# Input tile as the outer loop in the first output blocks behind five norms of a decoder step

## The chip, the cores and the metric

The kernel runs on one core of a Trainium2 chip. The metric is the device time of one execution in microseconds (us), lower is better; of several executions the median counts. All times "at" a point are us from the span's start in one profiled execution.

## The reference, cut to what matters

One inference step of a two-layer decoder for 512 prompt tokens and 64 sample tokens (8 sequences of 8), in float32, width 1024. The parts that the change touches are these matrix products, each behind a norm or a gate that makes its input:

```python
def rms_norm(x, g):
    xf = x.astype(jnp.float32)
    y = xf * lax.rsqrt(jnp.mean(xf * xf, axis=-1, keepdims=True) + EPS)
    return (y * g.astype(jnp.float32)).astype(x.dtype)
...
        x = x + rms_norm(sq_relu_mlp(h, W['w_up'][i], W['w_down'][i]), W['norm_ff_post'][i])
        x = x + jax.nn.sigmoid(x @ W['ple_gate'][i]) * (ple[i] @ W['ple_proj'][i])
...
    h = rms_norm(x, kv_in_g)
    ckr = h @ w_dkv
...
    cq = rms_norm(h @ w_dq, q_norm_g)
    q = (cq @ w_uq).reshape(B, T, N_HEADS, QK_NOPE + QK_ROPE)
```

The second layer's MLP is `square(relu(h @ w_up)) @ w_down` with 4096 hidden columns.

## The kernel before, in words

Activations lie with the feature on the partitions and the 576 tokens in the free dimension, as 8 tiles of 128 features, and the tokens are worked in two halves, h = 0 and 1, of 288. A **unit** is one output block: 128 output features of one half. Its product runs over the input tiles k (8, or 6 behind the query norm, where the rank is 768), and to keep float32 precision each k takes three matmuls (`three`, L2285 to L2290): weight high part by input high part, high by low, low by high. So a unit has 24 matmuls (18 behind the query norm, 12 in the MLP's down products).

TensorE works through all units in an order written out by hand. Before the change, most products run the units one after another, with k inside (`product`, L2318, and `up`, L2549). For the first unit that reads a new input, TensorE waits at each k for that tile's low part (`a_lo`); the later units find all tiles there. Two earlier places already have k as the outer loop over three units (`product_by_rows`, L2348, and `ff_up_by_rows`, L2468).

A unit starts when two more things are there:

- **Its bank.** Four PSUM banks serve the units in turn, so unit n waits until unit n - 4 has been read out by VectorE (`bank_free`). VectorE runs its own fixed order: for the gate units it is `gate` (L1954: sigmoid from ScalarE times an embedding, L1957, which frees the bank, then the addition to X, L1960), and in the MLP's up units the square of the relu (`u_square`, L1881, L1884). In that order stand also the updates of X (L1622) and the low parts of the next input (L1590, L1594).
- **Its weights.** A part of 128 weight columns (in the down products 256 columns of a shorter k) is split by ScalarE into its high part WH (L651) and by GpSimd into its low part WL (L1302). Four parts fit in the ring. The part for a later unit can be split only when the last unit that reads the old part in that slot has ended, and stands in the fixed order of ScalarE and GpSimd, among squares, sums and scalings of the norms.

Where weights serve both halves, the units come as groups: in the gate product units 0 to 3 are h 0 and 4 to 7 are h 1 of the same four parts, in dkv likewise, in dq units 0, 1 and 2, 3, in uq 0 to 3 and 4 to 7; in the MLP's up product 0 to 3 and 4 to 7. The `total` of a norm (L2309, L2315) is one matmul with a matrix of ones that sums the squares over the partitions. After it comes a root on ScalarE (L687), a reciprocal on VectorE (L1615 or L1610), scaling on GpSimd (L1338), the update of X (L1622) or nothing, the high part on ScalarE (L701, L703) and the low part on VectorE (L1590, L1594).

In the MLP, the chain of one up unit is: relu (ScalarE, L972), square (VectorE, L1884, frees the bank), high part (ScalarE, L976), low part (GpSimd, L1489). The buffer of the squares holds two, so the square of unit n waits for the low part of unit n - 2. For units 4 to 7 GpSimd does one weight part (L1302) and one low part (L1489) in turn.

Of the kernel before, what the change touches and what calls it, by code (L numbers as in the profile page):

```python
# [35 lines left out]
KT = D // P  # L36
TP, TS = 512, 64
T = TP + TS
H = T // 2
# [37 lines left out]
RAW0, DENSE0, UNIT0, UNITS = {}, {}, {}, {}  # L77
# [46 lines left out]
def slab_tiles(phase, j):  # L124

    return 8 if phase[:3] == "ple" else 1 if (phase, j) == ("dkv", 2) else 2


TILES = {p: [(h, j, t) for g in groups for h in range(2) for j in g for t in range(slab_tiles(p, j))]
         for p, groups in GROUPS.items()}  # L130
# [69 lines left out]
A = Order([(v, h, m) for v, h, n in SPLITS for m in range(n)])  # L200
# [19 lines left out]
BANKS = 4  # L220
# [21 lines left out]
def decoder_step(nc, io):  # L242
    with ExitStack() as ctx:
# [3 lines left out]
        def sem(name):  # L247
            return ctx.enter_context(nc.semaphore(name))

        bank = [ctx.enter_context(nc.psum_tensor(f"bank{i}", [P, 512], F32)) for i in range(8)]  # L250
# [57 lines left out]
        unit_done, bank_free = sem("unit_done"), sem("bank_free")  # L308
# [5 lines left out]
        a_hi, a_lo, x_done, sc_done = sem("a_hi"), sem("a_lo"), sem("x_done"), sem("sc_done")  # L314
# [5 lines left out]
        def half(t, m, h):  # L320
            return t[:, m, h * H:(h + 1) * H]
# [285 lines left out]
        def part_width(d):  # L607

            kt, n = slab_shape(*DENSE[d][1:])
            return kt, n // (PART0[d + 1] - PART0[d])  # L610
# [1673 lines left out]
        def _(pe):  # L2284
            def three(out, wsl, hl, first, last):  # L2285

                (wh, wl), (xh, xl) = wsl, hl
                nc.tensor.matmul(out, wh, xh, start=first, stop=False)  # L2288
                nc.tensor.matmul(out, wh, xl, start=False, stop=False)  # L2289
                return nc.tensor.matmul(out, wl, xh, start=False, stop=last)  # L2290

            def wpart(d, k, t):

                w = part_width(d)[1]
                q, c = divmod(t * P, w)
                r, a = (PART0[d] + q) % WRING, k * w + c
                return WH[:, r, a:a + P], WL[:, r, a:a + P]

            def rows(src, k, h):

                return half(src[0], k, h), half(src[1], k, h)

            def ready(d, t, i=None):
                w = PART0[d] + t * P // part_width(d)[1] + 1
                pe.wait_ge(lo_done, w if i is None else w + 2 * RING * i)

            Asrc, Bsrc = (AH, AL), (BH, BL)
# [10 lines left out]
            def product(phase, v, first=0, last=None, src=None):  # L2318

                kt = part_width(DENSE0[phase])[0]  # L2320
                for n, (h, j, t) in list(enumerate(TILES[phase]))[first:last]:
                    u, d = UNIT0[phase] + n, DENSE0[phase] + j
                    b = bank[u % BANKS][:, 0:H]
                    ready(d, t)
                    pe.wait_ge(bank_free, u + 1)
                    for k in range(kt):
                        if v and n == [x[0] for x in TILES[phase]].index(h):
                            pe.wait_ge(a_lo, A(v, h, k))
                        ins = three(b, wpart(d, k, t), rows(Asrc, k, h) if src is None else src(k, h), k == 0,
                                    k == kt - 1)  # L2330
                    ins.then_inc(unit_done, 1)
# [13 lines left out]
                        pe.wait_ge(lv_sq, m + 1)  # L2345
                        nc.tensor.matmul(dst, ones[:, :], LVS[:, m, :], start=first, stop=last).then_inc(lv_sum, 1)

            def product_by_rows(phase, v, units):  # L2348

                h = TILES[phase][0][0]  # L2350
                for k in range(KT):
                    pe.wait_ge(a_lo, A(v, h, k))
                    for n in range(units):
                        _, j, t = TILES[phase][n]
                        u, d = UNIT0[phase] + n, DENSE0[phase] + j
                        if k == 0:
                            ready(d, t)
                            pe.wait_ge(bank_free, u + 1)
                        ins = three(bank[u % BANKS][:, 0:H], wpart(d, k, t), rows(Asrc, k, h), k == 0, k == KT - 1)
                        if k == KT - 1:  # L2360
                            ins.then_inc(unit_done, 1)

            def turn_input(e):
# [181 lines left out]
            def mlp(layer):  # L2545
                phase, sty, stx, st = f"mlp{layer}", f"y{layer}", f"x{2 * layer + 1}", f"m{layer}"
                d0, u0, b0 = DENSE0[phase], UNIT0[phase], UP * NCH * layer

                def up(i, first, last):  # L2549
                    for n in range(first, last):  # L2550
                        h, j, t = n // 4, n % 4 // 2, n % 2
                        ready(d0 + j, t, i)
                        pe.wait_ge(bank_free, u0 + n + 1 + CHUNK * i)
                        for k in range(KT):
                            if type(i) is int and i == 0 and n % 4 == 0:
                                pe.wait_ge(a_lo, A(f"ff{layer}", h, k))
                            ins = three(bank[(u0 + n) % BANKS][:, 0:H], wpart(d0 + j, k, t), rows(Asrc, k, h), k == 0,
                                        k == KT - 1)
                        ins.then_inc(unit_done, 1)

                def down(i, first, last):
                    for n in range(first, last):
                        h, j, t = n // 8, 2 + n % 8 // 4, n % 4
                        ready(d0 + j, t, i)
                        pe.wait_ge(bank_free, u0 + UP + n + 1 + CHUNK * i)
                        for k in range(FC):
                            if n % 8 == 0:
                                pe.wait_ge(u_lo, b0 + up_n(h, k) + 3 + UP * i)
                            ins = three(bank[(u0 + n) % BANKS][:, 0:H], wpart(d0 + j, k, t), rows(Bsrc, k, h), k == 0,
                                        k == FC - 1)  # L2570
                        ins.then_inc(unit_done, 1)

                def turn_p(kt):
                    if kt == 0:
                        pe.wait_ge(p_in, 80 * (layer + 1))
                    else:
                        pe.wait_ge(p_lo, 6 * layer + 3)
                    for b in range(4):
                        nc.tensor.transpose(bank[6][:, b * P:(b + 1) * P], p_stage[:, b, kt * P:(kt + 1) * P],
                                            ident[:, :])  # L2580
                    nc.tensor.transpose(bank[7][:, 0:TS], p_stage[0:TS, 4, kt * P:(kt + 1) * P], ident[0:TS, 0:TS])\
                        .then_inc(p_turned, 1)

                up(0, 0, 2)
                total(sty, 1)
                up(0, 2, 8)
                down(0, 0, 16)
                with pe.Fori(1, NCH - 1) as i:
                    up(i, 0, 8)
                    down(i, 0, 16)  # L2590
                up(NCH - 1, 0, 8)
                down(NCH - 1, 0, 3)
                for h in range(2):
                    total(stx, h)
                down(NCH - 1, 3, 10)
                total(st, 0)
                turn_p(0)
                down(NCH - 1, 10, 13)
                turn_p(1)
                down(NCH - 1, 13, 16)  # L2600
                pe.wait_ge(p_lo, 6 * layer + 6)
                product(f"ple{layer}", None, src=lambda k, h: (BH[:, 2 * k + h, 0:H], BL[:, 2 * k + h, 0:H]))
                total(st, 1)

            product("gate0", "g0", 0, 1)
            total("m0", 1)
            product("gate0", "g0", 1)
            product("dkv", "kv", 0, 5)
            total("x2", 0)
            product("dkv", "kv", 5, 7)  # L2610
            total("x2", 1)
            product("dkv", "kv", 7)
            product("dq", "mx", 0, 1)
            for h in range(2):
                total("ck", h)
            product("dq", "mx", 1, 9)
            total("cq", 0)
            product("dq", "mx", 9)

# [14 lines left out]
                nc.tensor.transpose(bank[5][0:n, 0:DR], KR[0:DR, t0:t0 + n], ident[0:DR, 0:DR])\  # L2634
                    .then_inc(kv_turned, 1)

            product("uq", "cq", 0, 2)
            total("cq", 1)
            product("uq", "cq", 2, 4)
            pe.wait_ge(rope_in, 16)  # L2640
            pe.wait_ge(dve_step, KR_STEP)
            rot(0, KR)
            product("uq", "cq", 4, 8)
            for j in range(5):
                turn_kv(j)
                product("uq", "cq", 8 + 3 * j, 11 + 3 * j)
# [99 lines left out]
            for h in range(NH):  # L2746
                e = h % 2
                ins = nc.tensor.matmul(bank[5][:, h * TS:(h + 1) * TS], DUP[:, e, :],
                                       QR[:, h // 2, TP:T], start=True, stop=True)
# [32 lines left out]
            g0 = RAW0["cache"]  # L2782
# [122 lines left out]
            for hd in range(NH):  # L2905
# [5 lines left out]
                for k in range(4):  # L2911
                    a = k * 512 + (hd % 4) * P
                    ins = nc.tensor.matmul(bank[hd % 4][:, 0:TS], RAW[:, g % RING, a:a + P],
                                           LATS[:, k, hd].rearrange("p s t -> p (s t)"), start=k == 0, stop=k == 3)
# [74 lines left out]
```

## Time and profile before

| | |
|---|---|
| runs | 1956.98, 1959.21, 1967.64 us; median 1959.21 us |
| profiled execution | 1963.1 us, span 1960.8 us |
| TensorE (PE) busy | 91% of the span |
| GpSimd (POOL) busy | 52% |
| VectorE (DVE) busy | 47% |
| ScalarE (ACT) busy | 38% |
| mean granted TensorE clock | 0.952 of full |

A row of the timeline has the start, the duration, the engine, the line of the kernel, the operation, output and input tiles, how many instructions were merged, and in brackets the idle time of that engine just before with what ended it. PE rows of matmuls start 0.13 us apart when the engine runs without a pause at full clock; their durations overlap.

### The profile page before, as it was taken

How to read it: one execution, taken by the hardware profiler on the slowest of the kernel's cores; microseconds unless marked ns; L12 is line 12 of the kernel's file. 1: busy time of each engine (PE TensorE's matmuls, PEld its weight loads, DVE VectorE, ACT ScalarE, POOL GpSimd, SP SyncE). 2: the span in 40 equal slices, each digit the busy share in tenths (PEclk: the TensorE clock that was granted, in tenths of full speed). 3: DMA queues.
4: the chain of work that ended last, by engine and by line, in shares of the span. 5: the costliest groups of instructions: out<-in, count | busy, mean ns of one | idle time of the engine just before them, and what ended most of it. 6: DMA issues, size and time to landing. Idle time of an engine off the chain costs nothing.

```text
span 1960.8 us, 33358 instructions
## 1 busy us (share of the span) xinstructions
PE 1792.0 (91%) x12372; PEld 1609.7 (82%) x12372; DVE 923.3 (47%) x2170; ACT 739.9 (38%) x1454; POOL 1019.3 (52%) x739
## 2 busy tenths in 40 slices
PE   5994699999999799889999899999979999999978
PEld 4992699998899798888866566565969999999978
DVE  4687789943423325673344444444162222222283
ACT  4445444445444343632132333333232232322332
POOL 3784689986799784754210000000465555555662
PEclk9996899999999899998998899999889999999989
DMA  4521245544355341312102145555412222222201
GB/s 117 154 82 46 86 130 172 169 166 130 108 172 158 123 151 33 111 49 78 54 1 65 33 124 166 151 155 166 141 44 87 86 80 73 82 85 74 78 22 49
DMA packets 183288, 198.54 MB, mean 101 GB/s; under 512 B 32985, under 2 KB 138035, under 8 KB 183170
## 3 DMA queue, kind: packets, MB, share of 16 engines
q1 hardware_dynamic: 178144, 190.94, 31.5%
q10 hardware_dynamic: 5026, 6.02, 1.0%
q8 instruction: 75, 1.23, 0.3%
q14 instruction: 43, 0.35, 0.1%
HBM read 192.14 MB, written 4.79 MB: 100 GB/s over the span
## 4 chain that ended last, share of the span: by engine, by line
PE 66%; POOL 14%; DVE 11%; ACT 4%; issue 4%; DMA 1%; ACTq 0%; SPq 0%; POOLq 0%; DVEq 0%
PE bank L2288 16%; PE bank L2289 16%; PE bank L2290 16%; POOL WL L1302 7%; PE bank L2831 4%; PE bank L2865 3%; PE bank L2789 3%; DVE X L1622 2%; POOL acc L1328 2%; DVE AL L1590 2%; ACT WH L651 1%; PE bank L2730 1%; DVE AL L1594 1%; POOL R L1380 1%; PE bank L2711 1%
## 5 line engine op out<-in xcount | busy, mean ns | idle before, releaser
L1302 POOL TENSOR_TENSOR WL<-RAW,WH 128x1024 fp32r<-128x1024 f32 (+1 forms) x283 | 670.7, 2380 | 738.2 <-ACT WH L651 736.5
L2288 PE MATMUL bank<-AH,WH 128*128 128x288 f32 x2112 | 646.1, 306 | 65.4 <-DVE AL L1590 40.9
L2289 PE MATMUL bank<-AL,WH 128*128 128x288 f32 x2112 | 633.4, 300 | 0.0
L2290 PE MATMUL bank<-AH,WL 128*128 128x288 f32 x2112 | 632.6, 300 | 0.0
L2288 PEld LDWEIGHTS bank<-AH,WH 128*128 128x128 f32 x2112 | 406.9, 193 | 81.5 <-DVE AL L1590 36.5
L2289 PEld LDWEIGHTS bank<-AL,WH 128*128 128x128 f32 x2112 | 407.8, 193 | 0.9
L2290 PEld LDWEIGHTS bank<-AH,WL 128*128 128x128 f32 x2112 | 407.2, 193 | 0.0
L651 ACT ACTIVATE WH<-RAW 128x1024 fp32r<-128x1024 f32 (+1 forms) x283 | 293.5, 1045 | 301.3 <-PE bank L2290 283.9
L2288 PE MATMUL bank<-BH,WH 128*128 128x288 f32 (+1 forms) x1120 | 339.8, 303 | 25.6 <-DVE Y L1772 14.4
L2289 PE MATMUL bank<-BL,WH 128*128 128x288 f32 (+1 forms) x1120 | 336.1, 300 | 0.0
L2290 PE MATMUL bank<-BH,WL 128*128 128x288 f32 (+1 forms) x1120 | 336.0, 300 | 0.0
L2288 PEld LDWEIGHTS bank<-BH,WH 128*128 128x128 f32 x1120 | 213.2, 190 | 31.1 <-issue 27.7
L2289 PEld LDWEIGHTS bank<-BL,WH 128*128 128x128 f32 x1120 | 213.4, 191 | 1.4
L2290 PEld LDWEIGHTS bank<-BH,WL 128*128 128x128 f32 x1120 | 213.0, 190 | 1.5
L1699 DVE SCALAR_TENSOR_TENSOR bank<-S,taps,bank 128x224 f32<-128x224 f32 x464 | 134.8, 364 | 0.0
L1884 DVE TENSOR_TENSOR prod<-R,bank 128x288 f32<-128x288 f32 x64 | 29.1, 454 | 182.8 <-ACT R L972 111.2
L1893 DVE TENSOR_TENSOR Y<-Y,bank 128x288 f32<-128x288 f32 x112 | 50.7, 452 | 112.5 <-PE bank L2290 112.4
L1328 POOL TENSOR_TENSOR acc<-acc,sq 128x288 f32<-128x288 f32 x100 | 82.0, 823 | 32.5 <-ACT sq L669 26.7
L1338 POOL TENSOR_TENSOR scaled<-Y,R 128x288 f32<-128x288 f32 x76 | 69.2, 921 | 38.6 <-DVE X L1622 15.0
L1489 POOL TENSOR_TENSOR BL<-prod,BH 128x288 fp32r<-128x288 f32 x64 | 51.6, 811 | 61.0 <-ACT BH L976 61.0
L1772 DVE TENSOR_TENSOR Y<-Y,bank 128x288 f32<-128x288 f32 x112 | 49.5, 448 | 60.8 <-PE bank L2290 60.6
L2831 PE MATMUL bank<-Y,prod 128*64 128x256 f32 x640 | 76.1, 384 | 0.4 <-ACT Y L1212 0.4
(258 smaller groups left out, 2106.8 us busy)
## 6 DMA issues: line engine op xcount, KB each, us to landing
RAW<-in_w_up SPq DMA_DIRECT2D x48, 1024.0 KB, 5.5
RAW<-in_w_down SPq DMA_DIRECT2D x48, 1024.0 KB, 5.0
RAW<-in_cache_kv_latent SPq DMA_DIRECT2D x128, 256.0 KB, 2.8
RAW<-in_conv_pw SPq DMA_DIRECT2D x16, 512.0 KB, 7.5
RAW<-in_conv_pw SPq DMA_DIRECT2D x8, 1024.0 KB, 4.9
RAW<-in_ple_gate SPq DMA_DIRECT2D x8, 1024.0 KB, 5.0
RAW<-in_cache_k_rope SPq DMA_DIRECT2D x128, 32.0 KB, 2.8
RAW<-in_w_o SPq DMA_DIRECT2D x4, 1024.0 KB, 4.8
```

The lines of the kernel that those rows point to most:

```text
L651: nc.scalar.activation(split_part(WH, d, q), raw_part(d, q), ACT.Copy).then_inc(hi_done, 1)
L1302: nc.gpsimd.tensor_tensor(split_part(WL, d, q), raw_part(d, q), split_part(WH, d, q).bitcast(F32), ALU.subtract).then_inc(lo_done, 1)
L1328: nc.gpsimd.tensor_tensor(dst, dst, src, ALU.add).then_inc(acc_done, 1)
L1338: nc.gpsimd.tensor_tensor(scaled[:, SC(st, h, m) % 2, :], src, R2[:, h, :], ALU.mult).then_inc(sc_done, 1)
L1489: nc.gpsimd.tensor_tensor(half(BL, m, h), prod[:, n % 2, :], half(BH, m, h).bitcast(F32), ALU.subtract).then_inc(u_lo, 1)
L1699: nc.vector.scalar_tensor_tensor(out=run if c < CW - 1 else out, in0=src, scalar=w, in1=run, op0=ALU.mult, op1=ALU.add).then_inc(conv_late, 1)
L2288: nc.tensor.matmul(out, wh, xh, start=first, stop=False)
L2289: nc.tensor.matmul(out, wh, xl, start=False, stop=False)
L2290: return nc.tensor.matmul(out, wl, xh, start=False, stop=last)
L2789: ins = nc.tensor.transpose(bank[4 + c][:, q * P:(q + 1) * P], src[:, q * CL + c * P:q * CL + (c + 1) * P], ident[:, :])
L2831: ins = nc.tensor.matmul(bank[0][64 * g:64 * g + 64, 0:256], q, k, start=c == 0, stop=c == 4)
L2865: ins = nc.tensor.matmul(dst[g], SPT[:, k, 64 * g:64 * g + 64], src[:, b * CL:(b + 1) * CL], start=k == 0 and (j > 0 or g == 1), stop=k == 1)
```

## The change

`product_by_rows` gets a first unit and the right number of input tiles, and is used at five more call sites; the MLP of layer 1 gets a function of the same form, used twice. Around them the rest of each product is cut to fit. Two `total`s move: those of "ck" from behind dq unit 0 to behind dq unit 1, and that of "y1" half 1 from behind up unit 1 to behind up unit 2. Nothing changes on the other engines, and no instruction is added or taken away on TensorE.

```diff
-            def product_by_rows(phase, v, units):
-
-                h = TILES[phase][0][0]
-                for k in range(KT):
+            def product_by_rows(phase, v, units, first=0):
+
+                h, kt = TILES[phase][first][0], part_width(DENSE0[phase])[0]
+                for k in range(kt):
                     pe.wait_ge(a_lo, A(v, h, k))
-                    for n in range(units):
+                    for n in range(first, first + units):
                         _, j, t = TILES[phase][n]
                         u, d = UNIT0[phase] + n, DENSE0[phase] + j
                         if k == 0:
                             ready(d, t)
                             pe.wait_ge(bank_free, u + 1)
-                        ins = three(bank[u % BANKS][:, 0:H], wpart(d, k, t), rows(Asrc, k, h), k == 0, k == KT - 1)
-                        if k == KT - 1:
+                        ins = three(bank[u % BANKS][:, 0:H], wpart(d, k, t), rows(Asrc, k, h), k == 0, k == kt - 1)
+                        if k == kt - 1:
                             ins.then_inc(unit_done, 1)
...
+                def up_by_rows(first, units):
+                    h = first // 4
+                    for k in range(KT):
+                        pe.wait_ge(a_lo, A(f"ff{layer}", h, k))
+                        for n in range(first, first + units):
+                            j, t = n % 4 // 2, n % 2
+                            if k == 0:
+                                ready(d0 + j, t, 0)
+                                pe.wait_ge(bank_free, u0 + n + 1)
+                            ins = three(bank[(u0 + n) % BANKS][:, 0:H], wpart(d0 + j, k, t), rows(Asrc, k, h), k == 0,
+                                        k == KT - 1)
+                            if k == KT - 1:
+                                ins.then_inc(unit_done, 1)
...
-                up(0, 0, 2)
+                up_by_rows(0, 3)
                 total(sty, 1)
-                up(0, 2, 8)
+                up(0, 3, 4)
+                up_by_rows(4, 4)
                 down(0, 0, 16)
...
-            product("gate0", "g0", 1)
-            product("dkv", "kv", 0, 5)
+            product("gate0", "g0", 1, 4)
+            product_by_rows("gate0", "g0", 4, 4)
+            product("gate0", "g0", 8)
+            product_by_rows("dkv", "kv", 4)
+            product("dkv", "kv", 4, 5)
...
-            product("dq", "mx", 0, 1)
+            product_by_rows("dq", "mx", 2)
             for h in range(2):
                 total("ck", h)
-            product("dq", "mx", 1, 9)
+            product("dq", "mx", 2, 9)
...
-            product("uq", "cq", 0, 2)
+            product_by_rows("uq", "cq", 2)
             total("cq", 1)
...
-            product("uq", "cq", 4, 8)
+            product_by_rows("uq", "cq", 4, 4)
```

## Rows read from the trace of the kernel before

**Rows 1.** The page, busy time of each engine.
```profile
PE 1792.0 (91%) x12372; PEld 1609.7 (82%) x12372; DVE 923.3 (47%) x2170; ACT 739.9 (38%) x1454; POOL 1019.3 (52%) x739
```

**Rows 2.** Waits of PE: line, what it waited for, us in total, times, longest us.
```profile
PE bank L2288 <- DVE AL L1590: 40.9, 28, 8.2
...
PE bank L2288 <- DVE AL L1594: 13.0, 12, 5.5
```

**Rows 3.** Timeline of gate0: VectorE frees banks (L1957), PE, one GpSimd weight part.
```profile
747.67 0.53 DVE L1957 TENSOR_TENSOR R<-prod,S 128x288 f32<-128x288 f32 x1 [0.44 <-ACT prod L1046]
...
753.49 0.45 DVE L1957 TENSOR_TENSOR R<-prod,S 128x288 f32<-128x288 f32 x1
...
754.35 0.45 DVE L1957 TENSOR_TENSOR R<-prod,S 128x288 f32<-128x288 f32 x1
...
757.90 0.29 PE L2288 MATMUL bank<-AH,WH 128*128 128x288 f32 x1
...
759.54 2.39 POOL L1302 TENSOR_TENSOR WL<-RAW,WH 128x1024 fp32r<-128x1024 f32 x1 [0.83 <-ACT WH L651]
...
764.30 0.30 PE L2288 MATMUL bank<-AH,WH 128*128 128x288 f32 x1
```

**Rows 4.** Windows: us; busy PE, PEld, DVE, ACT, POOL; granted clock; DMA.
```profile
748.10:755.00 6.90, 4.95 (x18) 4.20 (x19) 6.66 (x15) 2.50 (x7) 1.89 (x2) 0.52 0.00 0
795.90:799.30 3.40, 3.25 (x14) 3.25 (x15) 3.40 (x6) 1.97 (x6) 2.34 (x4) 0.52 0.76 228
831.00:834.40 3.40, 3.40 (x24) 3.40 (x25) 3.30 (x9) 3.40 (x9) 0.00 (x0) 1.00 0.00 0
1441.00:1451.30 10.30, 6.17 (x25) 5.82 (x26) 5.73 (x7) 2.76 (x5) 6.76 (x5) 0.51 0.33 103
```

**Rows 5.** Timeline of dkv: last gate unit's bank freed, PE's longest wait, unit 4 starts.
```profile
794.33 0.40 PE L2288 MATMUL bank<-AH,WH 128*128 128x288 f32 x1 [2.72 <-DVE AL L1590]
...
794.63 0.44 DVE L1957 TENSOR_TENSOR R<-prod,S 128x288 f32<-128x288 f32 x1
...
807.82 0.29 PE L2288 MATMUL bank<-AH,WH 128*128 128x288 f32 x1
```

**Rows 6.** Timeline of dq: PE's first matmul.
```profile
831.00 0.37 PE L2288 MATMUL bank<-AH,WH 128*128 128x288 f32 x1 [2.91 <-DVE AL L1590]
```

**Rows 7.** Timeline of uq: PE's last wait, GpSimd, total, first wait of half 1, weight part, unit 8.
```profile
885.82 0.61 PE L2288 MATMUL bank<-AH,WH 128*128 128x288 f32 x1 [1.04 <-DVE AL L1590]
...
887.43 1.82 POOL L1302 TENSOR_TENSOR WL<-RAW,WH 128x768 fp32r<-128x768 f32 x1
...
891.02 0.56 PE L2315 MATMUL bank<-acc,ones 128*128 128x288 f32 x1
...
898.00 0.37 PE L2288 MATMUL bank<-AH,WH 128*128 128x288 f32 x1 [0.42 <-DVE AL L1590]
...
905.60 1.84 POOL L1302 TENSOR_TENSOR WL<-RAW,WH 128x768 fp32r<-128x768 f32 x1 [2.72 <-ACT WH L651]
...
912.57 0.40 PE L2288 MATMUL bank<-AH,WH 128*128 128x288 f32 x1
```

**Rows 8.** Timeline of the MLP's first chunk: GpSimd's weight parts and low parts, PE, a square.
```profile
1442.08 2.56 POOL L1302 TENSOR_TENSOR WL<-RAW,WH 128x1024 fp32r<-128x1024 f32 x1
...
1448.42 2.37 POOL L1302 TENSOR_TENSOR WL<-RAW,WH 128x1024 fp32r<-128x1024 f32 x1
...
1452.48 0.40 PE L2315 MATMUL bank<-acc,ones 128*128 128x288 f32 x1
...
1456.69 0.40 PE L2288 MATMUL bank<-AH,WH 128*128 128x288 f32 x1 [0.40 <-POOL WL L1302]
...
1464.47 0.45 DVE L1884 TENSOR_TENSOR prod<-R,bank 128x288 f32<-128x288 f32 x1 [0.47 <-ACT R L972]
...
1475.65 0.81 POOL L1489 TENSOR_TENSOR BL<-prod,BH 128x288 fp32r<-128x288 f32 x1
...
1482.74 0.29 PE L2288 MATMUL bank<-BH,WH 128*128 128x288 f32 x1
```

## The prediction

> **What bounds the kernel now.** I read the page first: TensorE is busy 91% of the span and no other engine over 52% [rows 1]. So the change can only give or take where TensorE stands still. The waits of TensorE say where that is: for low parts of inputs behind a norm or a gate it stood 40.9 + 13.0 us in 40 waits, the longest 8.2 us [rows 2]. The seven new calls stand at some of these waits. The idea of the change is plain in them: the first unit has 0.4 us of work per input tile (three matmuls, 0.13 us apart), and a group of four has 1.6 us.
>
> That is one half of the question. The other is what the later units of a group need at k = 0: a free bank and a weight part. Units one after another ask for these 3.2 us apart (24 matmuls), a group asks for all at once, before its second k. TensorE is in order, so one missing bank stops the whole group. So I read each site in the timeline of VectorE and GpSimd, and looked up when the bank and the part come. I call three matmuls a triple, 0.40 us.
>
> A third reading is the clock. After waits it stood at 0.51 to 0.52, that is 1.2 GHz: for 6.9 us in gate0, for 3.4 us in dkv after a wait of 2.72 us, for 10.3 us in the MLP. But in dq, after a wait of 2.91 us, it stayed at 1.00, or 2.4 GHz [rows 4 to 6]. A stretch of 3.4 us at 1.2 GHz loses about 1.5 us of work.
>
> **Gate0, units 4 to 7: +6.6 us.** Unit 5 needs unit 1's bank, unit 6 that of unit 2, unit 7 that of unit 3. VectorE frees them at 748.20, 753.94 and 754.80, because gate(1) stands behind four of the eight updates of X, and gate(2) and gate(3) behind all of them [rows 3]. So TensorE does three triples up to 754.4, and reaches the second k only after 754.9. From there it has 29 triples: 11.6 us, to 766.5. The long idle stretch before it puts some 3.4 us of that at 1.2 GHz: +1.5, to 768.0. Before, unit 8 started at 764.30 [rows 3]: +3.7. Then the weights: the four parts that this group reads are all in the ring, and are now freed within its last round. A unit's end to the new part in its place takes ScalarE and GpSimd 4.1 us (unit 5 ended at 757.90, its successor's part at 761.93 [rows 3]). Unit 4 ends 1.2 us before the group, so unit 8 waits 2.9 us. Before, this part came 5 us too early and cost nothing: the cover was units 5 to 7, which now end with unit 4. The later parts come every 2.4 us, faster than the 3.2 us of a unit.
>
> **Dkv, units 0 to 3: +0.4 us.** Unit 3 needs the bank of gate unit 15, free at 795.07 [rows 5]. 29 triples and the same slow stretch of 3.4 us give 808.2; before, unit 4 started at 807.82. The weights serve half 1 as well, so there is no refill.
>
> **Dq, units 0 and 1: 0.** The low parts come faster than TensorE uses them once the first is there at 831.00 [rows 6]: 0.3 us at most, and the waits that follow are for GpSimd's weight parts behind the "ck" norm. The two "ck" totals come 3 us later, but VectorE is still at its low parts then. With that cover gone it would cost up to 3 us.
>
> **Uq, units 0, 1 and 4 to 7: -5.6 us.** Here the banks come from plain copies and are free. In the first pair TensorE follows the low parts to 885.8 and needs two more triples: 886.6. Total "cq" 1 waits for GpSimd's last sum, 887.43 [rows 7], and runs at 887.6 instead of 891.02. Of these 3.4 us, units 2 and 3 lose 1.2: their parts are the two that GpSimd does from 887.43, ready at 889.3 and 891.1, so unit 3 ends at 894.2. VectorE copies it and comes to the first low part of half 1 at 895.4; before TensorE had it at 898.00 [rows 7]. Then 24 triples, 9.6 us, each k of 1.6 us above the 1.2 us between low parts: 905.0. The refill lag is about 3.1 us with these shorter parts (1.84 instead of 2.39 us), so unit 8 starts at 907.0, against 912.57 [rows 7]. GpSimd's and VectorE's work overlap more here; I take nothing for it, up to 2 us.
>
> **MLP, units 0 to 2 and 4 to 7: +8.1 us.** Unit 1 needs a weight part that GpSimd ends at 1444.64, unit 2 one that it ends at 1450.79 [rows 8], both behind the scalings of the norm in its order and independent of TensorE. So the second k starts after 1451; 22 triples from 1450.9 are 8.8 us, and the slow stretch 1.7 more (none, if the clock were up; 3, if it took the 6 us seen before 1451.3 [rows 4]): 1461.4. Total "y1" 1 ran at 1452.48: it is 8.9 us late. So is GpSimd's low part of unit 0 (it waits until ScalarE has had unit 1's end), and behind it the weight part of unit 3, which TensorE got at 1456.69. The norm's half 1 chain hangs on both, and moves by 8.4. Unit 7 needs unit 3's bank, whose square stands behind four updates of X: 1464.47 + 0.45 [rows 8], now 1473.3. From there 29 triples: 1484.9, against 1482.74: +2.2. The group takes back most of the delay. Then 2.9 for the refill as above. And a pile: for units 4 to 7 GpSimd does a weight part and a low part in turn, 2.37 + 0.81 us, and the square of unit 6 waits for the low part of unit 4, that of unit 7 for unit 5's. Counted from the group's end, weights are there at 2.9, low parts 3, 4, 5 at 3.7, 6.9, 10.1, so the banks of 6 and 7 are free at 7.4 and 10.6. The down units (1.6 us each) want them at 6.1 and, after that wait, 9.1: 1.4 + 1.6 = 3.0. Before, the squares ran 3.2 us apart and hid this.
>
> **Sum.** 6.6 + 0.4 + 0 - 5.6 + 8.1 = 9.5. The two refill waits of 2.9 us can bring a slow stretch: 0 by dq's wait, 1.5 to 1.7 by dkv's [rows 4 to 6]; I take 0.8 for each, since they are alike in length: 11.1 us. The profiled execution's 1963.1 becomes 1974.2; it is 3.9 above the median of 1959.2, so the forecast is 1970.3. A measurement here can tell some 0.5%, 9.8 us, from no change.
>
> **Rivals.** First, faster: banks and parts come in time, and each group runs without a stop. Gate0: 744.7 + 12.8 + 2.9 = 760.4, -3.9. Dkv: 789.8 + 12.8 = 802.6, -5.2. Uq -5.6. MLP: a total 3.5 earlier and a group like gate0's, -7.4. Together -22, 1937. It decides where the bank of unit n - 4 is free when the group starts. For it speak the 53.9 us of rows 2; against it the stamps 754.80, 795.07 and 1450.79. The Trainium skill, Perfetto Trace Analysis, Matmul Optimizations, wants matmuls back-to-back in batches; by that rule this rival comes true. The trace agrees in uq alone.
>
> Second, small: the order is as I say, but the clock stays up and the squares keep pace. Without the slow stretches (1.5, 1.5, 1.7, 1.6) and the pile (3.0) it is +1.8; with half of them, +6: 1961 to 1965. For it speaks dq's clock of 1.00 after 2.91 us.
>
> Third, uq gives nothing: its earlier totals meet GpSimd's work, or a later wait takes them back. Then the losses stand alone, +16.7, 1976. The Trainium skill, TensorE: Matmul & The Clock Gate, Loop structure matters more than you think, puts k inside and the outputs outside to keep matmuls dense; by that rule no group should gain. Against it: in uq, 24 triples took 13.1 us from 898.00 to the transposes before 912.57, 3.5 more than their work.
>
> **How the numbers follow.** Forecast 0.38, at 1970.3 (its own range 1966 to 1975); uq nothing 0.12; small 0.37; faster 0.13, which holds also gains smaller than -22. Slower is 0.50, same 0.37, faster 0.13. The range leaves out the faster rival and a little above: 1958 to 1978.
>
> **What would show it.** In gate0: a wait of the second and third triple for VectorE's L1957, and one of about 2.9 us for POOL WL L1302 at unit 8. In dkv one wait for L1957 of 3 to 4 us. In uq the total at about 3 us less behind unit 0's first k, and unit 8 some 5 us earlier in relation to it. In the MLP two waits for POOL WL in the first round, 9 and 6 us, the total some 9 us later, then waits for the squares, L1884, in the down units. I am wrong if TensorE's waits at L2288 for VectorE's low parts vanish with nothing in their place, or if the clock stays at 1.00 through the MLP's first rounds.

## The result and the profile after

The changed kernel took 1984.19 us (median of 4 runs, 1980.6 to 1986.34) beside 1961.72 us of the kernel before (4 runs): a ratio of 1.0116, with a 95% interval of 1.0086 to 1.0145. The forecast was 1970.3, with a range up to 1978. So the direction was right, and the loss was 22 us instead of 11. The two profiled executions lie closer together: 1980.6 against 1963.1, +17.5. In a later comparison with more runs (below, the changed kernel once more) the ratio was 1.0062, 1.0037 to 1.0086. These two intervals only touch, at 1.0086, and that is part of what had to be explained.

The page of the changed kernel, busy time and the granted clock over the span. TensorE is as busy as before [rows 1], within 3 us:

```profile
span 1978.3 us, 33358 instructions
PE 1794.8 (91%) x12372; PEld 1613.6 (82%) x12372; DVE 933.5 (47%) x2170; ACT 739.4 (37%) x1454; POOL 1018.5 (51%) x739
```

The waits of PE at the line of the products (what it waited for, us in total, times, longest):

```profile
PE bank L2288 <- POOL WL L1302: 32.8, 11, 9.5
PE bank L2288 <- DVE AL L1590: 21.0, 9, 8.4
...
PE bank L2288 <- DVE R L1957: 11.6, 4, 4.7
PE bank L2288 <- DVE AL L1594: 9.5, 7, 5.5
...
PE bank L2288 <- DVE prod L1884: 4.0, 3, 1.7
```

The change did what it says. The waits for low parts went from 53.9 us in 40 waits [rows 2] to 30.5 us in 16. In their place came 22.8 us more for weight parts (they were 10.0), 11.6 us for banks behind the gates' last step (L1957) and 4.0 us for banks behind the squares (L1884): 38.4 us for 23.4.

The sites, in PE's timeline: gate0 (three stops), dkv (two), dq:

```profile
747.23 0.58 PE L2288 MATMUL bank<-AH,WH 128*128 128x288 f32 x1 [3.08 <-DVE R L1957]
...
752.95 0.58 PE L2288 MATMUL bank<-AH,WH 128*128 128x288 f32 x1 [4.66 <-DVE R L1957]
...
769.84 0.41 PE L2288 MATMUL bank<-AH,WH 128*128 128x288 f32 x1 [2.68 <-POOL WL L1302]
...
798.60 0.37 PE L2288 MATMUL bank<-AH,WH 128*128 128x288 f32 x1 [0.70 <-DVE R L1957]
...
802.42 0.58 PE L2288 MATMUL bank<-AH,WH 128*128 128x288 f32 x1 [3.19 <-DVE R L1957]
...
839.74 0.61 PE L2288 MATMUL bank<-AH,WH 128*128 128x288 f32 x1 [2.81 <-DVE AL L1590]
```

Then uq (its total and its two stops for weight parts), and in the MLP's first chunk the stops of units 1, 2, 3 and 7 and of the first down unit:

```profile
896.89 0.75 PE L2315 MATMUL bank<-acc,ones 128*128 128x288 f32 x2 [0.66 <-POOL acc L1328]
...
898.65 0.40 PE L2288 MATMUL bank<-AH,WH 128*128 128x288 f32 x1 [1.01 <-POOL WL L1302]
...
916.20 0.40 PE L2288 MATMUL bank<-AH,WH 128*128 128x288 f32 x1 [1.06 <-POOL WL L1302]
...
1454.94 0.61 PE L2288 MATMUL bank<-AH,WH 128*128 128x288 f32 x1 [9.50 <-POOL WL L1302]
...
1461.06 0.61 PE L2288 MATMUL bank<-AH,WH 128*128 128x288 f32 x1 [5.03 <-POOL WL L1302]
...
1476.62 0.40 PE L2288 MATMUL bank<-AH,WH 128*128 128x288 f32 x1 [3.37 <-POOL WL L1302]
...
1484.45 0.37 PE L2288 MATMUL bank<-AH,WH 128*128 128x288 f32 x1 [1.66 <-DVE prod L1884]
...
1498.96 0.40 PE L2288 MATMUL bank<-BH,WH 128*128 128x288 f32 x1 [2.68 <-POOL WL L1302]
```

And the clock (window; busy time of the engines; granted clock; DMA), in gate units 8 and 9, behind dkv's waits and behind dq's:

```profile
771.30:774.30 3.00, 3.00 (x15) 3.00 (x14) 3.00 (x2) 0.25 (x1) 3.00 (x2) 0.51 0.18 41
798.60:807.00 8.40, 5.21 (x22) 5.01 (x23) 8.37 (x12) 6.26 (x15) 5.39 (x5) 0.68 0.37 118
839.70:846.00 6.30, 6.26 (x26) 6.27 (x27) 6.16 (x14) 3.77 (x9) 0.00 (x0) 0.51 0.00 0
```

Now the time between like points of the two timelines. Each shift is taken against the point before it:

| stretch, up to | before | after | shift in it | forecast |
|---|---|---|---|---|
| total "m0" | 734.16 | 733.07 | -1.1 | 0 |
| gate unit 8 | 764.30 | 769.84 | +6.6 | +6.6 |
| gate units 8 to 15 (clock) | | | +1.65 | +0.8 |
| dkv's group | | | +1.6 | +0.4 |
| dq, to total "cq" 0 | 867.78 | 878.52 | +1.9 | 0 |
| uq unit 8 | 912.57 | 916.20 | -7.1 | -5.6 |
| first page transposition, behind the attention heads | 1121.11 | 1131.49 | +6.8 | 0 |
| MLP, first unit | 1434.60 | 1444.88 | -0.1 | 0 |
| MLP, ninth down unit | 1495.39 | 1514.58 | +8.9 | +8.1 and +0.8 (clock) |
| end | | | -1.7 | 0 |

Eight of the ten lines are within 1.7 us of the forecast, and dq is 1.9 off. The one that stands out, +6.8 us, is in the attention heads, between two stages that the change touches: not one instruction is changed there.

### The profile page after: what moved, and what is told of

Same layout as the page of the kernel before. It is cut to its first block, busy times and chain, and to the rows that moved or that the text cites. A ratio compares the mean times of both kernels' runs of the same rounds, so it can differ in the third digit from the quotient of the medians.

```text
span 1978.3 us, 33358 instructions
## 1 busy us (share of the span) xinstructions
PE 1794.8 (91%) x12372; PEld 1613.6 (82%) x12372; DVE 933.5 (47%) x2170; ACT 739.4 (37%) x1454; POOL 1018.5 (51%) x739
## 4 chain that ended last, share of the span: by engine, by line
PE 66%; POOL 14%; DVE 10%; issue 4%; ACT 4%; DMA 1%; ACTq 0%; SPq 0%; POOLq 0%; DVEq 0%
PE bank L2288 16%; PE bank L2290 16%; PE bank L2289 16%; POOL WL L1302 8%; PE bank L2849 4%; PE bank L2883 3%; PE bank L2807 3%; POOL acc L1328 2%; DVE X L1622 2%; ACT WH L651 1%; PE bank L2748 1%; PE bank L2729 1%; POOL R L1380 1%; DVE AL L1590 1%; DMA RAW<-in_conv_pw 1%
## 5 line engine op out<-in xcount | busy, mean ns | idle before, releaser
L651 ACT ACTIVATE WH<-RAW 128x1024 fp32r<-128x1024 f32 (+1 forms) x283 | 293.2, 1044 | 296.3 <-PE bank L2290 277.8
L1884 DVE TENSOR_TENSOR prod<-R,bank 128x288 f32<-128x288 f32 x64 | 29.0, 453 | 193.5 <-ACT R L972 119.4
L972 ACT ACTIVATE R<-bank 128x288 f32<-128x288 f32 x64 | 26.3, 411 | 135.9 <-PE bank L2290 135.9
```

The source lines that it names most:

```text
L651: nc.scalar.activation(split_part(WH, d, q), raw_part(d, q), ACT.Copy).then_inc(hi_done, 1)
```

## First look: each part of the change alone

Four kernels, each with some of the new calls and the others as before. Uq alone:

```diff
-            product("uq", "cq", 0, 2)
+            product_by_rows("uq", "cq", 2)
...
-            product("uq", "cq", 4, 8)
+            product_by_rows("uq", "cq", 4, 4)
```

> Only the two groups of uq (units 0 and 1, units 4 to 7) are kept; the other five calls are undone. Theory A (the sites add up, and the 6.6 us lost between the first rope rotation and the cache pages came from where the clock and GpSimd's parts happened to fall): unit 8 of uq starts 5.6 to 7 us earlier behind total cq 0 than before, the attention heads take what they took before (954.90 to 1121.11, 166.2 us) or up to 7 us more by chance, time -7 to 0 us. Theory B (earlier totals of uq disturb the heads): the heads take 173 us, time about 0. Theory C (a group costs by itself, by switching bank at every triple): triples in the groups are longer than 0.40 us, time above before.

Measured: 1963.61 us, ratio 0.9999 (0.998 to 1.0018). In its trace, unit 8 comes 5.7 us earlier behind total "m0" than before (172.7 us against 178.4), as forecast. The heads take as much back: 172.5 us from the last projection of uq to the first page transposition, where the kernel before takes 1121.11 - 954.90 = 166.2. By itself this is theory B's picture; the kernels below decide against it.

What uq gains is less TensorE's idle time than its clock. Windows from total "cq" 0 to unit 8, the kernel before and this one:

```profile
867.78:912.57 44.79, 39.28 (x229) 35.94 (x229) 22.74 (x35) 13.96 (x25) 26.59 (x24) 0.85 0.21 44
```
```profile
867.98:907.06 39.08, 34.55 (x230) 32.01 (x230) 23.27 (x35) 13.78 (x25) 23.22 (x23) 0.96 0.21 41
```

Idle time (window less PE busy) went from 5.5 to 4.5 us, the busy time for the same matmuls from 39.3 to 34.6, at a mean clock of 0.85 and 0.96. So 1.0 of the 5.7 us are stops, and 4.7 are matmuls that run faster.

Gate0 alone:

```diff
-            product("gate0", "g0", 1)
+            product("gate0", "g0", 1, 4)
+            product_by_rows("gate0", "g0", 4, 4)
+            product("gate0", "g0", 8)
```

> Only the group of gate0 units 4 to 7 is kept. Theory A: three stops in it, of 3 and 4.7 us for L1957 and of 2.7 us for GpSimd's part at unit 8, a slow stretch after the first two and perhaps one after the third: +6.6 to +8.3 us at dkv, and that to the end: ratio 1.0034 to 1.0042. Theory C: more than that, in every triple. If a later stage takes the delay back: 0.

Measured: 1968.99 us, ratio 1.0036 (1.0017 to 1.0055), heads 166.2 us. Its three stops are those of the full change: 3.08, 4.67 and 2.68 us.

The MLP alone:

```diff
-                up(0, 0, 2)
+                up_by_rows(0, 3)
                 total(sty, 1)
-                up(0, 2, 8)
+                up(0, 3, 4)
+                up_by_rows(4, 4)
```

> Only the two groups of the MLP are kept. Theory A: stops of 9.5, 5.0, 3.4, 1.7, 2.7, 1.1 and 1.3 us as in the changed kernel, down unit 8 starts 8.9 us later behind the end of w_o than before, ratio 1.0045, heads unchanged. If the loss in the heads belongs to none of the sites, 0 to 7 us more by chance.

Measured: 1969.75 us, ratio 1.0039 (1.0018 to 1.0061), heads 170.8 us, and in the MLP the same stops within 0.03 us (9.50, 5.03, 3.37, 1.63, 2.67). Its heads are long as well, though nothing ahead of them differs from the kernel before.

Dkv and dq alone:

```diff
-            product("dkv", "kv", 0, 5)
+            product_by_rows("dkv", "kv", 4)
+            product("dkv", "kv", 4, 5)
...
-            product("dq", "mx", 0, 1)
+            product_by_rows("dq", "mx", 2)
             for h in range(2):
                 total("ck", h)
-            product("dq", "mx", 1, 9)
+            product("dq", "mx", 2, 9)
```

> Only the groups of dkv (units 0 to 3) and dq (units 0 and 1) are kept. Theory A: dkv 0.4 to 1.6 us, dq 0 to 2 us by how the clock falls, since a stop of 3 us for L1957 and one of 2.8 us for the low part each may or may not bring a slow stretch: +1 to +4 us, ratio 1.0005 to 1.002. With the clock at full the ck totals come 3 us late without a price; at half clock they come 6 us late and delay the norm by 2.

Measured: 1966.75 us, ratio 1.0015 (0.9997 to 1.0033), heads 171.8 us.

The four ratios add up to +0.89% (-0.01 + 0.36 + 0.39 + 0.15). So there is no cost that only the whole change has, beyond what the intervals allow, and the groups do not cost by themselves: a triple takes 0.40 us in them as elsewhere at full clock. The question was left with the heads. They took 166.2 us in two of the six traces and 171 to 173 in four, two with uq's calls and two without. So uq's earlier totals (theory B) are not what makes them long.

## What decides the heads: a near tie on a shared port

In heads 2 and 4 (counted from 0, so the third and the fifth) GpSimd makes two late weight parts back to back. In the middle of that, VectorE scales the softmax rows (L2112), on which TensorE waits. Both engines, kernel before, third head (start, duration, engine, line, operation; an entry of x2 holds two instructions):

```profile
1022.47 4.96 POOL L1302 TENSOR_TENSOR WL<-RAW,WH 128x1024 fp32r<-128x1024 f32 x2 [64.50 <-ACT WH L651]
1024.73 0.49 DVE L2112 TENSOR_SCALAR scaled<-scaled,tiny 128x512 f32<-128x512 f32 x1
...
1025.27 0.66 PE L2720 MATMUL bank<-ident,scaled 128*128 128x128 f32 x4 [0.49 <-DVE scaled L2112]
```

The same place in the changed kernel:

```profile
1026.52 2.00 ACT L651 ACTIVATE WH<-RAW 128x1024 fp32r<-128x1024 f32 x2
...
1027.65 4.65 POOL L1302 TENSOR_TENSOR WL<-RAW,WH 128x1024 fp32r<-128x1024 f32 x2 [66.09 <-ACT WH L651]
...
1028.89 0.70 ACT L1165 ACTIVATE scaled<-bank,tiny 128x512 f32<-128x512 f32 x1
...
1029.91 2.68 DVE L2112 TENSOR_SCALAR scaled<-scaled,tiny 128x512 f32<-128x512 f32 x1
...
1032.64 1.12 PE L2738 MATMUL bank<-ident,scaled 128*128 128x128 f32 x4 [2.68 <-DVE scaled L2112]
```

In both, VectorE's row starts 2.26 us behind the start of GpSimd's pair, 0.06 us before the row of the second part. Before, it got in between (0.49 us, and the pair took 4.96 us, 0.31 more than 4.65). After, it came in behind the second: 1029.91 + 2.68 = 1032.59, and the pair ended at 1032.30. The Trainium skill, SBUF — State Buffer, SBUF: two separate sides, says that the port pair these two engines share is an exclusive lock and the loser fully blocks. The rows agree with blocking; that a waiting instruction may or may not get in between two of the other engine's is not in it. I call it a tie, won if VectorE gets in between and lost if it waits for the second part.

The meeting itself is no accident. Both engines are released by ScalarE, in its fixed order: GpSimd by the end of the first WH part (L651), VectorE by the exponentials two instructions behind the second (L1165). In all ten traces that have the pairs, 20 meetings, the distance is 2.25 or 2.26 us; 7 were won and 13 lost. What decides one is below what the rows resolve.

The lost tie costs 2.2 us at once. Here it cost more behind, where TensorE's clock was slow. Windows of 11 us behind the tie, the kernel before and the changed kernel:

```profile
1025.00:1036.00 11.00, 10.73 (x53) 7.56 (x54) 5.25 (x19) 3.34 (x10) 2.43 (x1) 1.00 0.01 1
```
```profile
1032.00:1043.00 11.00, 10.36 (x28) 6.72 (x29) 3.43 (x13) 2.21 (x6) 0.30 (x1) 0.61 0.01 1
```

Over the whole of the heads, TensorE's idle time is 2.2 us longer in the changed kernel (15.0 and 12.8) and the busy time for the same 608 matmuls 4.6 us (140.8 and 136.2): together the 6.8.

The test takes the pair apart. The same four parts, one in each of heads 1 to 4:

```diff
-                if hd in (2, 4):
-                    hi_next(2)
+                if hd in (1, 2, 3, 4):
+                    hi_next(1)
```

First in the kernel before:

> The kernel before, but the four late weight parts that ScalarE and GpSimd make in heads 2 and 4 (two back to back) are made one in each of heads 1 to 4. The arithmetic is the same. Theory P (a near tie on the port that VectorE and GpSimd share decides the heads' length: in a head with two GpSimd parts back to back, VectorE's sum scaling either gets in between them, 0.49 us, or waits for the second, 2.68 us, and a wait of TensorE is followed by slower clock): VectorE's scaling waits no longer behind a second part, none of the heads' scalings is above about 1.5 us; the heads' part from the last projection of uq to the first page is 164 to 167 us (166.2 before), and the time is within 0.3% of before (1956 to 1966 us). Theory Q (the heads' length varies by itself, with the clock, whatever GpSimd does): this kernel's heads lie anywhere from 166 to 173 us, no shorter than those of other kernels.

Measured: 1960.14 us (12 runs, 1958.35 to 1963.45), ratio 0.9995 (0.9985 to 1.0004), heads 164.7 us. Its third head:

```profile
1024.77 2.35 POOL L1302 TENSOR_TENSOR WL<-RAW,WH 128x1024 fp32r<-128x1024 f32 x1 [16.80 <-ACT WH L651]
1026.88 0.52 DVE L2112 TENSOR_SCALAR scaled<-scaled,tiny 128x512 f32<-128x512 f32 x1
...
1027.45 0.66 PE L2720 MATMUL bank<-ident,scaled 128*128 128x128 f32 x4 [1.08 <-DVE scaled L2112]
```

No scaling in the heads took over 0.52 us. The spread of its 12 runs is as telling as the median: 5.1 us, where 20 runs of the kernel before on the same chip went from 1955.40 to 1968.38.

Then uq's two calls with the pair taken apart:

> The two uq groups of the change alone, with the late weight parts made one a head as in the kernel beside it. Theory P: the uq gain of 5.6 us is now kept: heads 164 to 167 us as there, and the time is 5 to 6 us under the kernel beside it (ratio to before 0.996 to 0.998). Theory Q: nothing is kept, heads 170 us and more, ratio to before 1.000, and the same time as the kernel beside it or more.

Measured: 1954.36 us, ratio 0.9967 (0.9951 to 0.9983), 5.8 us under the kernel beside it, as theory P said. The heads were 162.7 us, a little under the range that it gave. So uq's gain is real, and it reaches the time when the heads do not take it back.

The changed kernel, once as it is and once with the pair taken apart. (These texts count the heads from the first matmul on the norm's roots, 17.2 us further on: the 166.2 us of before are 149.0 so.)

> The changed kernel once more, for its time beside the others of this chip: 1980 to 1987 us. Theory P (the near tie on the shared port is lost once more in head 2 than before): its third head's scaling takes 2.68 us again, heads (last projection of uq to first page) 155 to 156 us against 149. Theory Q: the heads may be short this time, with the same kernel.

> The changed kernel with the late weight parts made one in each of heads 1 to 4 instead of two in heads 2 and 4. Theory P: no scaling of 2.68 us, heads 146 to 148 us, and 6 to 9 us under the changed kernel beside it (it gets rid of both lost ties): about 1976 us, ratio to before 1.006 to 1.009, which is near what was forecast for the change as a whole (9.5 + 1.6 us). Theory Q: as the changed kernel beside it, within 2 us.

Measured: as it is 1976.36 us (11 runs, 1973.94 to 1986.29), ratio 1.0062 (1.0037 to 1.0086), under the 1980 to 1987 that I had written; in its trace both ties are lost again (2.68 and 2.67 us), the heads 155.7 us. Taken apart: 1972.08 us (12 runs, 1969.78 to 1976.44), ratio 1.0036 (1.0014 to 1.0057), no scaling over 0.52 us, heads 147.6 us. The spans are 1980.6 and 1972.8, 7.8 us apart, within the 6 to 9 expected. The medians are 4.3 us apart and the ratio of 1.0036 lies under the 1.006 to 1.009 expected, so the forecast by medians was a miss. The 11 runs of the kernel as it is fall in two groups, four from 1982.9 to 1986.3 (the profiled one is among them) and seven from 1973.9 to 1979.6. That would fit runs that lose their ties and runs that win one or both; it is not shown, as only the profiled executions show a tie.

The 14 traces side by side; heads counted in this second way, the two scalings at GpSimd's pairs in order:

| kernel | scaling, head 2 | head 4 | heads |
|---|---|---|---|
| before; gate0 alone | 0.49 | 2.68 | 149.0; 149.1 |
| dkv and dq alone | 0.49 | 2.68 | 154.6 |
| MLP alone; its half 1 alone | 2.68; 2.69 | 2.68; 2.69 | 153.7; 153.7 |
| uq alone; changed, twice | 2.68 | 2.68 | 155.3; 155.8, 155.7 |
| dq alone; three groups (below) | 0.49 | 0.49 | 146.4; 146.5 |
| pair taken apart, four kernels | | | 145.5 to 147.6 |

All traces without a lost tie lie at 145.5 to 147.6 us, all with one or two at 149.0 to 155.8. Kernels with the very same program up to the heads (before, MLP alone, its half 1 alone) stand on both sides in head 2. So the tie is decided by something other than the calls of the change. Theory Q has its part too: with the ties the same, the heads took 149.0 and 154.6 us. In dkv and dq's trace the clock was 0.69 from 1022 to 1033 us, right behind a tie that it had won, where the kernel before has 1.00; what brought it down there stays open.

## Which calls gain, and how large a group may be

The change's own losses stand where a group asks for a bank or a part that is not there. If so, the same change with smaller groups, at the sites where TensorE waits for low parts alone, must gain:

```diff
-            product("dkv", "kv", 0, 5)
+            product_by_rows("dkv", "kv", 3)
+            product("dkv", "kv", 3, 5)
...
-            product("uq", "cq", 0, 2)
+            product_by_rows("uq", "cq", 2)
...
-            product("uq", "cq", 4, 8)
+            product_by_rows("uq", "cq", 4, 4)
...
                 up(0, 0, 2)
                 total(sty, 1)
-                up(0, 2, 8)
+                up(0, 2, 4)
+                up_by_rows(4, 3)
+                up(0, 7, 8)
```

> Only groups whose stages the traces show waiting for the norm's tiles rather than for weight parts: both uq groups as in the change, dkv with three units in the group instead of four (units 0 to 2), and in the MLP the group of four on the second half of the chunk alone (first three units of it), its first two units one by one as before; gate0 and dq as before. Theory A (each site's time is the wait it takes away less the weight parts and banks that it wants earlier, and the sites add): uq gives 5.6 us and the heads take about as much back, dkv and the MLP group of this size lose or give under 2 us, since the weight parts of the second half are made by then: 1957 to 1966 us. Rival (a group of row order by itself costs time wherever it stands): slower than before by 2 us and more.

Measured: 1948.89 us, ratio 0.9936 (0.992 to 0.9952). That is below the range that I gave (1957 to 1966). Dkv's group of three gives 3.2 us (dq's first matmul comes 93.6 us behind total "m0", not 96.8), and the MLP's three units 3.9 (from the first stop for a low part in its first chunk to the ninth down unit 54.5 us, not 58.4). I had written under 2 us for these. (In the seven traces in which this stretch of the MLP is as before it took 57.7 to 58.5 us.) As in uq, a part of the gain is clock: in dkv idle time and busy time each fell by 1.6 us, in the MLP idle time by 0.7 and busy time by 3.2, with the clock at 0.91 instead of 0.82. Both ties of the heads were won in its trace. The stops of the group of three in dkv and of the next stage, then those of the MLP from unit 4 on:

```profile
790.46 0.37 PE L2288 MATMUL bank<-AH,WH 128*128 128x288 f32 x1 [0.71 <-DVE R L1957]
...
826.84 0.58 PE L2288 MATMUL bank<-AH,WH 128*128 128x288 f32 x1 [3.55 <-DVE AL L1590]
```
```profile
1458.34 0.40 PE L2288 MATMUL bank<-AH,WH 128*128 128x288 f32 x1 [0.48 <-DVE AL L1590]
...
1469.87 0.37 PE L2288 MATMUL bank<-BH,WH 128*128 128x288 f32 x1 [1.09 <-DVE prod L1884]
```

The same with GpSimd's pair taken apart:

> The kernel beside it with the late weight parts made one a head. Theory P: heads 164 to 167 us, so 5 to 6 us under the kernel beside it, 1951 to 1960 us. Theory Q: the same time as the kernel beside it.

Measured: 1947.28 us, ratio 0.993 (0.9914 to 0.9947), heads 164.7 us. It lies below the range of 1951 to 1960 us, and theory P's distance to the kernel beside it (5 to 6 us) was a miss: it is 1.6 us, which is as near to theory Q's. That kernel's trace had won both ties, so this pair of kernels does not tell the theories apart. With the runs of the two overlapping, either may be the best version, 12.5 and 14 us under the kernel before.

The second group of the MLP alone, with four units as in the change:

```diff
-                up(0, 2, 8)
+                up(0, 2, 4)
+                up_by_rows(4, 4)
```

> Of the change only the MLP's second group, all four units of the chunk's second half; its first group is left as before. Theory A1 (the loss of 8.9 us is all of the first group, which wants weight parts that GpSimd has not made): from the first group's start to the first down product it gains as the kernel with three units did, 3 to 4 us, no stop on a weight part over 1 us: 1956 to 1960 us. Theory A2 (the fourth unit waits for its bank, as the fourth of dkv did): it gains under 1 us or loses.

Measured: 1963.42 us, ratio 0.9996 (0.9972 to 1.002). Theory A2 holds. The fourth unit stops the group, and there is a second stop at the first down unit, which the group of three does not have (the rows above):

```profile
1458.55 0.58 PE L2288 MATMUL bank<-AH,WH 128*128 128x288 f32 x1 [2.34 <-DVE prod L1884]
...
1475.40 0.40 PE L2288 MATMUL bank<-BH,WH 128*128 128x288 f32 x1 [2.67 <-POOL WL L1302]
```

To the ninth down unit it takes 59.5 us: 1.1 more than before and 5.0 more than with three units. In dkv the step from three to four is alike: four units lose 0.4 us in the kernel with dkv and dq alone (dq's first matmul 97.2 us behind total "m0") and 1.6 in the whole change, three gain 3.2. So of the MLP's 8.9 us some 7.8 would be its first group's (8.9 - 1.1), which wants weight parts that GpSimd has yet to make; that group was not run alone.

Last, the pair of dq alone:

> Of the change only the pair of dq. Theory A: the same wait at its start (2.8 us), the totals of ck come 5 us later, and the norm behind them is late by no more than the slack that it has: 0 to +2 us on the way to the totals of cq. Rival: the pair costs nothing by itself and the 2 us seen in the changed kernel came from dkv's group ahead of it: 0 within 0.5 us.

Measured: 1962.29 us, ratio 1.0001 (0.9974 to 1.0029). From its first stop (830.27, 2.81 us) to total "cq" 0 it takes 36.85 us; before it was 36.78. The totals of "ck" come 3.0 us later behind the stop (836.70 - 830.27 against 834.43 - 831.00), not the 5 that I wrote, and nothing behind them is late. In the kernel with dkv and dq it is 36.84. So the 1.9 us of the changed kernel are not the pair's, nor dkv's. They come with the clock, which stood at 0.51 for 6.3 us behind the same wait in the changed kernel (above), and here stayed up:

```profile
830.30:836.60 6.30, 6.30 (x48) 6.30 (x49) 6.16 (x14) 3.71 (x9) 0.00 (x0) 1.00 0.00 0
```

The totals of "ck" then came 9.2 us behind the stop (848.96 - 839.74), and the norm behind them was late. This is no accident of one execution: all three traces of the changed kernel (one of them with the pair of the heads taken apart) have 0.51 there behind 2.81 or 2.82 us, all eight without gate0's group and with a stop of 2.8 to 2.9 us have 1.00, and gate0 alone, which has not even the pair of dq, has 0.73. So gate0's group goes with the slower clock; how it brings the clock down 70 us later was not tried.

## Why the prediction was wrong

**Gate0, +6.6: right**, and by its mechanism: two stops for L1957, 3.08 and 4.66 us, and 2.68 for the weight part where 2.9 was forecast. The slow clock behind that wait was taken at 0.8 us, a mean of "0 by dq's wait, 1.5 to 1.7 by dkv's". It took 1.65, the upper of the two.

**Dkv, +0.4:** the stop was forecast (3 to 4 us, measured 3.19), its price was short by 1.2 us. The step "the same slow stretch of 3.4 us" failed: two stops in a row left the clock at 0.68 on average for 8.4 us. Of the sites this has the plainest lesson: I accepted four units and worked out what the fourth costs, and did not see that it was all of the cost.

**Dq, 0:** right for the pair as such (36.85 against 36.78 us). The sentence "with that cover gone it would cost up to 3 us" came true in the changed kernel, +1.9, by slow clock and not by the pair.

**Uq, -5.6:** right alone by its stamps (total "cq" 1 3.4 us earlier, unit 8 5.7), -7.1 in the changed kernel. But the sum has no term for the clock here, and 4.7 of the 5.7 us are clock. The stamps were worked out at full clock and held against a stretch that ran at 0.85, so the number came out right without its main reason. The 1.4 more in the changed kernel are clock as well (idle 4.5 us in both, clock 1.00 against 0.96), not the overlap for which "I take nothing for it, up to 2 us". The third rival's "24 triples took 13.1 us" is a slip: from 898.00 to the transposes at 911.84 it is 13.8, of which 1.5 are stops and the rest beyond 9.6 is slow clock.

**MLP, +8.1:** 8.9, with the stops forecast as 9 and 6 at 9.50 and 5.03, and the total "y1" 9.8 us late instead of 8.9. The refill wait was 2.68, and the pile 1.10 + 1.28 instead of 1.4 + 1.6.

**The heads, no term at all: wrong.** This is the step that failed. The sum treated all between uq and the MLP as moved and not changed. The third rival had "its earlier totals meet GpSimd's work, or a later wait takes them back", at +16.7; the profiled executions gave +17.5. But its reason was only half right: uq's totals are not the cause. The heads lost 6.8 us in that trace, 2.2 by a tie which the kernel before had won in its own trace (the two kernels with its program up to there each lost it) and 4.6 by slower clock. Without the heads the two profiled executions are 17.5 - 6.8 = 10.7 us apart, and the sum had 11.1; that it came so near is in part luck, as the misses of the sites (uq -1.5, dq +1.9, the clock and dkv +2.1, the stretches outside -2.9) cancel. The number to hold against the forecast of 11.1 is that with the tie taken out of both kernels: the spans differ by 1972.8 - 1960.0 = 12.8 us, the ratios by 1.0036 - 0.9995 = 0.41%, 8 us, with an uncertainty of some 4.5. The rest of the 22 us is the heads' and what four runs can tell; how much each has is open. How often each kernel loses its ties was not counted, since only profiled executions show it.

Of the two rules that the prediction weighed, the one on batches (the Trainium skill, Perfetto Trace Analysis, Matmul Optimizations) came true at no site with four units whose banks were busy, but did in uq and in the groups of three, where no unit waited longer than 0.71 us for a bank. By the other (the Trainium skill, TensorE: Matmul & The Clock Gate, Loop structure matters more than you think) no group should gain; the kernel with three groups, 0.9936, shows otherwise.

## What to carry to other kernels

Before several output blocks are run side by side, look up for each block when its bank and its weights come free, and stop at the block before the first that would wait: one block too many turned 3 to 4 us of gain into a loss of about 1, twice. When you price such a group, price the clock with the stops: in uq 1.0 us of the gain was idle time and 4.7 clock. Look also for places where two engines that share a port always meet at the same moment: here such a place moved the profiled time by several us between kernels whose programs are the same up to it, and moving one instruction apart narrowed the spread of the runs before it made anything faster. And compare a part of a change in its own stretch of the trace first; the medians of four runs each said 22 us, where the sites held 11.

## What was new about the hardware

A VectorE instruction from SBUF to SBUF that comes just as one GpSimd instruction ends and the next is ready is either served in between (0.49 us) or blocked for all of the second (2.68 us). Both happened at the same distance in the rows, 2.25 to 2.26 us behind the start of the pair: 7 of 20 times in between, 13 times blocked.

The granted clock behind a like wait went here with what lies further ahead, and repeated with it: behind 2.8 to 2.9 us at dq's start it was 1.00 for 6.3 us in eight traces without gate0's group, 0.73 with that group alone, and 0.51 in all three of the changed kernel.
